# The down maps of two feed-forward layers as seven products of quarters in place of eight, on one Trainium2 core

## What is computed

```python
def swiglu(h, w_gate, w_up, w_down):              # first block, D_FF = 2816
    return (jax.nn.silu(h @ w_gate) * (h @ w_up)) @ w_down

u = jnp.square(jax.nn.relu(hf @ w_up[l])) @ w_down[l]     # second block, D_FF_2 = 4096
x = x + rms_norm_2(u, post_ffn_g[l])
```

## Time and profile before

| | us |
|---|---|
| median of 3 runs | 3475.19 |
| the 3 runs | 3471.4, 3475.19, 3580.33 |
| the profiled execution, own time | 3467.81 |
| its span, first to last instruction | 3466.0 |
| PE busy | 3338.5 (96%) |
| DVE busy | 1966.1 (57%) |
| ACT busy | 1478.7 (43%) |
| mean granted TensorE clock | 0.982 of full speed |

### The profile page before, as it was taken

How to read it: one execution, slowest core, us unless ns; L and a number is a source line. 1 busy time by engine, 2 the same in 40 slices (tenths; PEclk the granted TensorE clock), 3 DMA queues, 4 the chain that set the end, 5 groups by cost and what they waited for, 6 DMA issues and landing times.

```text
span 3466.0 us, 42731 instructions
## 1 busy us (share of the span) xinstructions
PE 3338.5 (96%) x16754; PEld 2620.5 (76%) x16754; DVE 1966.1 (57%) x3296; ACT 1478.7 (43%) x2665; POOL 0.2 (0%) x4
## 2 busy tenths in 40 slices
PE   8989999999999999999999998898999999999998
PEld 7456666788888878888886687777874788888787
DVE  3545767566656546655555766555544475544454
ACT  2214555553333345533335544444421465544443
POOL 0000000000000000000000000000000000000000
PEclk9999999999999999999999999999999999999999
DMA  6410000232222466433334000000022523346665
GB/s 258 182 43 1 0 1 13 79 110 73 80 85 85 136 230 212 147 104 113 104 106 147 16 19 13 7 25 1 1 85 86 188 96 105 107 143 203 220 201 177
DMA packets 251320, 346.76 MB, mean 100 GB/s; under 512 B 11376, under 2 KB 141040, under 8 KB 247920
## 3 DMA queue, kind: packets, MB, share of 16 engines
q1 hardware_dynamic: 251120, 344.04, 30.2%
HBM read 276.88 MB, written 67.11 MB: 99 GB/s over the span
## 4 chain that ended last, share of the span: by engine, by line
PE 88%; DVE 7%; ACT 2%; DMA 1%; issue 1%; SPq 0%; DVEq 0%; ACTq 0%
PE ps L199 86%; DVE M L2844 1%; DMA wr<-in_w_down 1%; PE ps L1236 1%; DVE NM L2093 1%; PE ps L703 1%; DVE QT L2112 0%; DVE RT L2111 0%; DVE QT L2114 0%; PE ps L2537 0%; ACT L2967 0%; ACT L2965 0%; DVE Pl L2087 0%; PE ps L234 0%; ACT M L2789 0%
## 5 line engine op out<-in xcount | busy, mean ns | idle before, releaser
L387 DVE TENSOR_TENSOR wl<-wr,wh 128x512 fp32r<-128x512 f32 x782 | 509.8, 688 | 600.6 <-ACT wh L363 598.1
L363 ACT ACTIVATE wh<-wr 128x512 fp32r<-128x512 f32 x782 | 455.2, 623 | 658.0 <-PE ps L199 529.1
L199 PE MATMUL ps<-ffn_h,wh 128*128 128x512 f32 x2176 | 671.5, 390 | 4.1 <-DVE Y L451 2.4
L199 PEld LDWEIGHTS ps<-ffn_h,wh 128*128 128x128 f32 x2176 | 408.7, 188 | 90.5 <-DVE Y L451 3.4
L199 PE MATMUL ps<-ffn_h,wl 128*128 128x512 f32 x1088 | 423.8, 390 | 0.0
L199 PE MATMUL ps<-in_h,wh 128*128 128x512 f32 x1200 | 370.0, 389 | 1.5 <-DVE Yf L451 1.5
L199 PE MATMUL ps<-wh,wh 128*128 128x512 f32 x864 | 338.2, 391 | 9.6 <-DVE wl L387 9.6
L199 PE MATMUL ps<-wl,wh 128*128 128x512 f32 x864 | 337.7, 391 | 0.0
L199 PE MATMUL ps<-wh,wl 128*128 128x512 f32 x864 | 337.3, 390 | 0.0
L199 PE MATMUL ps<-M,M 128*128 128x128 f32 (+1 forms) x2176 | 296.0, 296 | 36.6 <-DVE ybT L3006 16.6
L199 PEld LDWEIGHTS ps<-M,M 128*128 128x128 f32 (+1 forms) x2176 | 277.0, 202 | 56.8 <-DVE ybT L3006 17.9
(11 more groups left out here) (343 smaller groups left out, 5009.6 us busy)
## 6 DMA issues: line engine op xcount, KB each, us to landing
wr<-hid SPq DMA_DIRECT2D x108, 512.0 KB, 3.9
wr<-in_w_down SPq DMA_DIRECT2D x108, 512.0 KB, 4.6
wr<-in_w_up SPq DMA_DIRECT2D x54, 512.0 KB, 5.4
hid<-ob SPq DMA_DIRECT2D x108, 256.0 KB, 2.3
wr<-in_w_in SPq DMA_DIRECT2D x42, 512.0 KB, 5.2
kept<-ob SPq DMA_DIRECT2D x84, 256.0 KB, 2.0
late<-in_w_ada SPq DMA_DIRECT2D x16, 1024.0 KB, 7.3
wr<-in_w_out SPq DMA_DIRECT2D x32, 512.0 KB, 4.3
```

Of the source, the lines that this page charges most:

```text
L199: return e.op.matmul(out, left, right, start=start, stop=stop, skip_group_check=True)
L363: e.op.activation(self.rows(s)[0], src, ACT.Copy).then_inc(*e.event(self.name + "_act", ("w_high", self.name, s)))
L387: e.op.tensor_tensor(lo, src, hi.bitcast(F32), ALU.subtract).then_inc(*e.event(self.name + "_dve", ("w_low", self.name, s), *done))
```

## The change

`Down` takes the place of `Rows` for the two down maps (`Rows` stays for the output maps). The left operand (hidden, by token half and even or odd tile of a pair) and the right (weights, by odd or even tile and column half) are each taken as four quarters; seven products of sums of quarters, p1 to p7, give the four quarters of the output.

- **Parts.** A product runs over parts of two pairs. With one tile of each pair in a product, a part of two has two left slots and two right slots and 24 matmuls, as a pair had before. The first block has 6 parts, the last of one pair (12 matmuls); the second has 9, of which the second and the last have one pair.
- **Right sums.** In p1 the weights are loaded into tiles `T` (one of 128x1024 for each part) that lie where the up map's operand was. In p5, p6 and p4 DVE makes T = loaded - T before the splits, in p7 loaded = T - loaded.
- **Left sums.** For pairs that the up map makes by products, DVE makes s1 to s4 in the up map's stage (4 sums a pair, `sum_block`) and SP stores them beside the quarters. For the pairs made plainly (2 in the first block, 3 in the second: the first part, or the first two) the sums are made during the down map, in `S`.
- **Ends.** p1 and p5 are copied out by ACT; p6 is added onto p1's banks. DVE adds what a product contributes: 4 instructions of 128x512 at p6's end, 8 at p7's, 4 at each of p4, p3 and p2. The squares are then taken from `Y` (`square_row`), and the gain is multiplied in by 8, 4 and 4 instructions (`by_gain`).
- **Plan.** The first half's norm and addition to `X` lie between the parts of p3, the transposes for what follows (`middle`) at parts 1 and 2 of p2.
- **X.** `x_back` issues one 1 MB load in each of the first four parts of p6.

```diff
+    def ask_at(self, place, sem, holder, src, k, c, first, after=None):
+        n = len(self.asks)
+        self.asks.append((src, k, c, after, first, place, sem, self.holder.get(holder)))
+        self.holder[holder] = n
+        return n
...
+    def slot_sum(self, e, s):
+        out, left, right, op, ready = self.sums[s]
+        n, j, last = self.slots[s]
+        e.wait_ge(("raw", self.name, n), *ready)
+        done = [("raw_done", self.name, n)] if last and s in self.kept else []
+        e.op.tensor_tensor(out, left, right, op).then_inc(*e.event(self.name + "_dve", ("slot_sum", self.name, s), *done))
     def vector(self, e, upto):
         for s in self.ahead(e, upto, len(self.slots)):
+            for x in self.lead.get(s, []):
+                self.slot_sum(e, x)
             if isinstance(self.slots[s][0], int):
-                n, j = self.slots[s]
-                self.split(e, s, *([("raw_done", self.name, n)] if j else []))
+                n, j, last = self.slots[s]
+                self.split(e, s, *([("raw_done", self.name, n)] if last and s not in self.kept else []))
                 continue
...
+    def square_row(self, e, cb, t, before):
+        e.wait_ge(("whole", self.name, cb, t), before)
+        at = self.parts(t // 4, cb)[:, t % 4:t % 4 + 1]
+        e.op.activation(self.junk[:, 0:512], self.Y[:, t, 512 * cb:512 * cb + 512], ACT.Square, accum_out=at).then_inc(
+            *e.event(self.name + "_act", ("squared", self.name, t, cb)))
+    def by_gain(self, e, cb, t, group):
+        e.wait_ge(("squared", self.name, t, cb))
+        y = self.Y[:, t, 512 * cb:512 * cb + 512]
+        e.op.tensor_tensor(y, y, self.gain[:, 512 * cb:512 * cb + 512], ALU.mult).then_inc(*e.event(self.name + "_dve", ("read", group)))
...
+class Down:
+    ORDER = ("p1", "p5", "p6", "p7", "p4", "p3", "p2")
+    BANKS = {"p1": 4, "p5": 0, "p6": 4, "p7": 0, "p4": 4, "p3": 0, "p2": 4}
+    LEFT = {"p1": "a11", "p5": "s1", "p6": "s2", "p7": "s3", "p4": "a22", "p3": "s4", "p2": "a12"}
+    LEFT_SUM = {"p5": ("a21", "raw", ALU.add, True), "p6": ("a11", "kept", ALU.subtract, True), "p7": ("a22", "raw", ALU.subtract, False),
+                "p3": ("a12", "raw", ALU.subtract, False)}
+    RIGHT = {"p1": (0, 0, None), "p5": (0, 1, ("raw", ALU.subtract, True)), "p6": (1, 1, ("raw", ALU.subtract, True)),
+             "p7": (0, 0, ("kept", ALU.subtract, False)), "p4": (1, 0, ("raw", ALU.subtract, True)), "p3": (1, 1, None), "p2": (1, 0, None)}
+    def __init__(self, k, name, up, w, Y, end, store, stream, free):
+        self.k, self.name, self.up, self.Y, self.end, self.store, self.stream, self.free = k, name, up, Y, end, store, stream, free
+        pairs, made = w.shape[0] // 256, up.made
+        self.parts = [range(j, min(j + 2, made)) for j in range(0, made, 2)] + [range(j, min(j + 2, pairs)) for j in range(made, pairs, 2)]
+        self.kept = {("b", g): k.sb("T", [128, 1024], o) for g, o in zip(range(len(self.parts)), (32, 36, 48, 52, 40, 44, 56, 60, 28))}
+        self.kept.update({("a", g): k.sb("S", [128, 1024], 4 * g) for g in range((made + 1) // 2)})
+        self.at, self.slot, self.kept_by, first = len(stream.slots), {}, {}, None
+        for i, what in enumerate(self.ORDER):
+            for g, part in enumerate(self.parts):
+                at = self.slot[i, g] = len(stream.slots)
+                lead = stream.lead[at] = []
+                self.add_left(what, g, part, lead)
+                self.add_right(what, g, part, w, lead)
+        self.upto = len(stream.slots)
+        end.groups = lambda t: [self.row(cb, t) for cb in range(2)]
+        self.marks = {(5, n): n for n in range(end.PORTIONS)}
+        self.middle_at = {(6, 1): 0, (6, 2): 1}
+    def add_left(self, what, g, part, lead):
+        stream, n = self.stream, len(part)
+        sums = self.LEFT_SUM.get(what) if part[0] < self.up.made else None
+        load = lambda x: (self.up.hidden_parts(x, part), n, 512, len(stream.slots), self.up.parts_stored(x, part))
+        if what == "p5" and sums:
+            self.kept_by["a", g] = [("raw", stream.name, stream.ask_at(self.kept["a", g], f"rawT{g % 2}", ("T", g % 2), *load("a22")))] * 2
+        ask = stream.ask(*load(sums[0] if sums else self.LEFT[what]))
+        self.add_slots(ask, n, ("a", g), sums[1:] if sums else None, lead)
+    def add_right(self, what, g, part, w, lead):
+        stream, n = self.stream, len(part)
+        q, cb, sums = self.RIGHT[what]
+        src = w[256 * part[0]:256 * (part[0] + n), 512 * cb:512 * cb + 512].rearrange("(k h p) n -> p h k n", h=2, p=128)[:, q, :, :]
+        load = (src, n, 512, len(stream.slots))
+        if what == "p1":
+            last = ("product", self.up.name, "p1" if g < 4 else "p2" if g < 8 else "p4", self.up.pairs - 1)
+            ask = stream.ask_at(self.kept["b", g], f"rawT{g % 2}", ("T", g % 2), *load, last)
+        else:
+            ask = stream.ask(*load)
+        at = self.add_slots(ask, n, ("b", g), sums, lead)
+        if what == "p1":
+            self.kept_by["b", g] = [("w_low", stream.name, at + j) for j in range(n)]
+    def add_slots(self, ask, n, key, sums, lead):
+        stream = self.stream
+        at = stream.add_group(ask, n)
+        for j in range(n if sums else 0):
+            first, op, keep = sums
+            raw, kept = stream.half(ask, j), self.kept[key][:, 512 * j:512 * j + 512]
+            stream.sums[at + j] = (kept if keep else raw, raw if first == "raw" else kept, kept if first == "raw" else raw, op, [self.kept_by[key][j]])
+            self.kept_by[key][j] = ("w_low", stream.name, at + j)
+            if keep:
+                stream.kept.add(at + j)
+            lead.append(at + j)
+        return at
...
+            elif what == "p7":
+                e.wait_ge(("v", name, j))
+                self.count(e, e.op.tensor_tensor(self.part_of(1, j), self.part_of(1, 4 + j), src, ALU.add), ("whole", self.end.name, 1, j))
+                self.count(e, e.op.tensor_tensor(part, part, src, ALU.add), ("u7", name, j), ("read", self.group("p7", j)))
+            else:
+                cb, t = self.at_row(what)
+                e.wait_ge({"p4": ("u7", name, j), "p3": ("v", name, j), "p2": ("p1_copied", name, j)}[what])
+                self.count(e, e.op.tensor_tensor(part, part, src, ALU.add), ("whole", self.end.name, cb, t + j), ("read", self.group(what, j)))
+                if what == "p2" and j:
+                    self.by_gain(e, 0, 3 + j)
+        if what == "p4":
+            for j in range(4):
+                self.by_gain(e, 1, j)
+            for j in range(4):
+                self.by_gain(e, 0, j)
+        elif what == "p3":
+            for j in range(4):
+                self.by_gain(e, 1, 4 + j)
+        elif what == "p2":
+            self.by_gain(e, 0, 7)
...
+    def sync(self, e, x_back):
+        self.stream.sync(e, self.at + 8)
+        for i in range(len(self.ORDER)):
+            for g in range(len(self.parts)):
+                self.stream.sync(e, self.slot[i, g] + self.stream.SLOTS + 4)
+                if (i, g) == (0, 2):
+                    self.up.store_last_sums(e)
+                if i == 2 and g < 4:
+                    x_back(e, g)
...
+    AT = {"p1": ("s3",), "p2": ("s1",), "p3": ("s2", "s4")}
...
+    def sum_block(self, e, b):
+        x, j = b
+        left, right, op = {"s1": ("a21", "a22", ALU.add), "s2": ("s1", "a11", ALU.subtract), "s3": ("a11", "a21", ALU.subtract), "s4": ("a12", "s2", ALU.subtract)}[x]
+        left, right = self.key(left, j), self.key(right, j)
+        e.wait_ge(("final", self.name, left), ("final", self.name, right), ("final", self.name, ("s3", j)) if x == "s1" else None)
+        o = self.out(b) if x == "s1" else self.claim(e, b)
+        e.op.tensor_tensor(o, self.out(left), self.out(right), op).then_inc(*e.event(self.name + "_dve", ("final", self.name, b)))
...
-    def x_back(self, e):
+    def x_back(self, e, tp):
 
         v = self.k.d["spill"].rearrange("(t p) n -> p t n", p=128)
         e.wait_ge(("product", self.up.name, "p4", self.up.pairs - 1), *self.before.stored())
-        for tp in range(4):
-            e.op.dma_start(self.end.X[:, 2 * tp:2 * tp + 2, :], v[:, 2 * tp:2 * tp + 2, :]).then_inc(*e.load(f"x{tp}", ("x_back", self.up.name, tp)))
+        e.op.dma_start(self.end.X[:, 2 * tp:2 * tp + 2, :], v[:, 2 * tp:2 * tp + 2, :]).then_inc(*e.load(f"x{tp}", ("x_back", self.up.name, tp)))
```

More of the change, by code:

```diff
@@ L293, in __init__ @@
         self.slots = []
+        self.sums, self.lead, self.kept = {}, {}, set()
+        self.holder, self.turn = {}, 0
     def ask(self, src, k, c, first, after=None):
-        self.asks.append((src, k, c, after, first))
-        return len(self.asks) - 1
+        r = self.turn % self.RAWS
+        self.turn += 1
+        return self.ask_at(self.raw[r], f"raw{r}", r, src, k, c, first, after)
+    def ask_at(self, place, sem, holder, src, k, c, first, after=None):
[3 more added lines that the diff above has]
+        return n
```

(16 more changed lines are left out.)

215 lines of the change are left out of this document (183 added, 32 removed).

## The result

The change makes the kernel faster by 0.3%, far less than the 2% that one would act on: ratio to before 0.9972, 95% interval 0.9960 to 0.9984, which is 9.7 us of 3475.3. (In five of its ten executions, and in one of ten of before, all of the kernel ran some 110 us longer at a lower clock, so the plain median of 3521.54 us says nothing of the change, and no ratio counts such runs.) The other five took 3460.6 to 3469.5 us. The forecast was 3452, that is 15.7 us less than before's profiled execution.

A forecast was written before the change was run, and what follows sets the result against it. PE's matmuls and waits were taken as the bound: 3466.0 - 73.4 - 14.0 + 15.7 + 32.6 + 4.4 + 12.0 + 1.0 + 2.0 + 4.0 = 3450.3, plus 1.8 around the span, taken as 3452 us; range 3398 to 3492.

The forecast's parts named there:

- the left sums in the up maps: Up maps: 4 DVE instructions, 2.7 us, for a pair taking 19 or 38 us of matmuls; costed at nothing.
- What follows the first down map: After the first down map: its follower waited 1.5 us for `Yf`; banks are read sooner now, left in the bounds.
- 324 matmuls, 73.4 us: Down maps: 84 matmuls a pair instead of 96 over 27 pairs, at 0.2267 us each, saving 73.4 us.
- 14.0 us at X: Both down maps: PE's waits at X's loads and the lower clock behind them, 7.0 us each, wholly regained.
- The round: p5, p6, p7, p4: left split, right load, sums and splits, next right load; 6.65 us a part, PE needs 5.44.
- the term of 48.3 us: Down maps: time added by late parts in four products, 15.7 us in the first map and 32.6 in the second.
- rival 1: Down maps: short rhythm, the right load lands in 3.2 us, period 5.8 us; 3413 us in all, chance 0.15.
- Ends of products and clock: Down maps: p6 and p7 ends 2.2 us a map, p4's end 6.0 a map, lower clock 4.0 in all.
- The 2.0 us for SP: Both down maps: SP's waits to load `T` stand before the last stores of `hid`; 2.0 us, 0 to 6.
- 2 (no round): Down maps: the round does not bind, through overlap or DVE keeping its lead; 3388 us, chance 0.16.
- 3: Down maps: longer round, weights land in 4.7 us and X's loads add to it; 3486 us, chance 0.17.
- rival 4: Four products of the down maps: clock falls and stays, under 0.82; 3546 us at 0.65, 3680 at one half; chance 0.06.

The follow-up runs named there:

- e4: The change with s4 and the result behind it swapping places in the second up map; ratio to before 0.9940.
- f2: The change with e1's and e4's edits, plus at p2's end the adds before the gains and four splits fewer ahead of them; ratio to before 0.9763.
- e3: The kernel before with only X's four loads issued one each at pairs 2 to 5 of step 1; ratio to before 0.9957.
- f3: f2 with four of p4's eight gains made between its parts; ratio to before 0.9756, median 3389.0 us.
- e2: The change with X's four loads issued together in p6's first part; ratio to the kernel before 1.0006.
- e1: The change with a part's right sums made just ahead of its right slots, behind its left splits; ratio to before 0.9814, median 3408.1 us.

## Why the forecast was off, and what of it was right

- **The step that failed: the left sums in the up maps, costed at nothing.** I weighed the amount of DVE's work and not what its list waits for: a sum that claims a place waits for a store, and whatever stands behind it is late. The second up map took 8.6 us more, and e4 gives all of it back.
- **What follows the first down map, left in the bounds as a small gain.** It cost 4.7 us: the four adds that free the banks stand among splits and gains (f2). The end behind the last matmul cost 2.0, forecast 1.0. So outside the down maps 15.3 us were lost where the sum had 1.0.
- **324 matmuls, 73.4 us**: right. With X's part (about 15 us by e3) 88 us are to be had, and f3 has 85.
- **14.0 us at X**: right (15 by e3's ratio and 13.9 by its down maps, 12 to 14 by e2, each with its own neighbours).
- **The round**: right in kind; the chain shows it link by link, and e1 takes it away. The period was forecast as landing and 2.60 and is landing and 2.55. The landing was off: 4.05 taken, 3.5 and 3.6 measured in the two maps,

```profile
wr<-in_w_down SPq DMA_DIRECT2D x22, 512.0 KB, 3.5
wr<-hid SPq DMA_DIRECT2D x21, 512.0 KB, 4.6
...
wr<-hid SPq DMA_DIRECT2D x29, 512.0 KB, 4.4
wr<-in_w_down SPq DMA_DIRECT2D x29, 512.0 KB, 3.6
```

  so the term of 48.3 us was too large by some 23 (46 rounds of 0.5), and rival 1 was half right.
- **Ends of products and clock**: too small. 20.4 us were forecast (4.4, 12.0 and 4.0). With rounds at about 25 us, an estimate, what e1 gave back beyond them is some 30. The forecast had one wait of 1.2 us in every part, some 45 in all, and let a low clock be absorbed by them. But the 22 waits came in lumps behind p5, p6, p7 and p4, up to 5.7 us, and PE had no spare time behind them. About 15 us at the lower level is read from the stretches.
- **Luck in the maps**: these two errors, 23 us too much and some 15 too little, have no common cause and nearly cancel. 240 and 348 were forecast, 234.5 and 344.0 measured, 9.5 us better. The 2.0 us for SP in them is measured by no run.
- **Rivals**: 2 (no round) is refuted by the chain. It priced the time without the round at some 80 us under before's profiled execution, and f3, where the round is gone, is 85 under before. 3 and 4 did not come: the medians of the weights' landings stayed far from 4.7, and the clock did not stay low. (The seven stretches that rival 4 draws on average a clock of 0.88, not 0.83. And the 12 instructions of the earlier trace rows multiply PSUM by the gain, they do not add; the adds here take 0.68 us each, so nothing changes by it.)
- The class, within 2%, was right, and the time of the undisturbed runs lies in the range. The gain was 0.28% where 0.45% was forecast against the profiled execution's own time: by stages 11.5 of 15.7 us, since the 14.3 us more outside the maps outweigh the 9.5 that the maps did better (4.8, for a gap of 4.2; the rest is rounding). The other 1.8 us, down to the ratio's 9.7, lie within its interval. Against the median of before, 3452 would be a gain of 23 us; 7.4 of them are there only because the sum starts from an execution that was that much under the median.

The Trainium skill (DMA: Bandwidth & Descriptors, Anatomy of one DMA) gives its rule, about 2.0 us and the bytes at 436 GB/s, for a transfer that is issued through GpSimd, and the loads here go from SyncE. For 512 KB it is an estimate of 3.2 us: the weights' medians of 3.5 and 3.6 lie between it and the 4.05 that I took, and those of `hid`, 4.4 and 4.6, above both.

## What to carry to other kernels

When a step is added between a load and the release of the buffer that the next load needs, write the round down (release, load, sum, split, release) and compare it with what PE needs for a step; enough idle time on every engine doesn't help against it, but the order of two groups of instructions may. An instruction that waits for a store or a load holds everything behind it on its engine (in the up map 31.1 us of waits of DVE, 6.5 of PE behind them), so look at what its neighbours free. And once one engine had lost its lead here, the bursts at the boundaries showed too, with the clock behind them; with the lead given back (e1) they hardly did.

## What was not expected of the hardware

Of two loads issued one after the other, the first took about 1 us less, whichever it was: before, `hid` took 3.9 and the weights behind it 4.7; in the change the weights go first and take 3.5 or 3.6, `hid` 4.6 or 4.4. It is not so in every kernel, since in e1 both took 4.2 (second map, from issue to landing), and no run changed the order of the two alone:

```profile
wr<-hid SPq DMA_DIRECT2D x32, 512.0 KB, 4.2
wr<-in_w_down SPq DMA_DIRECT2D x31, 512.0 KB, 4.2
```

And waits of PE that are much shorter than the 4.7 us at X before brought stretches at 1.2 GHz, but not each time. In the first map the start of one matmul to that of the next was 2.60 us at 1309 us, and the mean clock there fell to 0.92, while 1.58 us at 1241 left it at 1.00. In the second, 2.58 us at 3229 left it at 1.00, and so did 2.17 at 3252 and 3.98 at 3262. So the length of the wait alone does not tell; what does is not shown here (columns as in the earlier trace rows).

```profile
1232.00:1246.00 14.00, 12.80 (x57) 10.30 (x56) 10.62 (x18) 6.50 (x12) 0.00 (x0) 1.00 0.62 207
...
1300.00:1322.00 22.00, 19.79 (x80) 15.66 (x79) 15.02 (x25) 7.88 (x16) 0.00 (x0) 0.92 0.53 180
...
3229.00:3242.00 13.00, 10.09 (x44) 7.80 (x43) 7.85 (x13) 4.99 (x10) 0.00 (x0) 1.00 0.55 192
...
3252.00:3275.00 23.00, 17.63 (x77) 13.99 (x76) 17.31 (x29) 10.53 (x20) 0.00 (x0) 1.00 0.52 172
```
